# A decoder step on one Trainium2 core: the conditioning products in four column strips, their weight slots spread over the stream

## The chip, the cores and the metric

The kernel runs on one core of one Trainium2 chip. The metric is the device time of one execution in microseconds. Engines are named as the profile names them: PE (TensorE matmul; PEld its weight loads), DVE (VectorE), ACT (ScalarE), POOL (GpSimd), SP (SyncE, which issues most transfers).

## What is computed

One step of a two-layer decoder over 256 prompt tokens and 8 single-token samples (T = 264 columns), model width 1024, all in fp32. Cut to what matters here:

```python
def trunk(x, c, ret_state, past, p):
    for l in range(DEPTH):                                   # DEPTH = 2
        sh1, sc1, g1, sh2, sc2, g2 = adaln(c, p['w_mod'][l], p['b_mod'][l], 6)   # silu(c) @ w + b
        if l < N_A_LAYERS:                                   # layer 0: retention
            h = modulate(rmsnorm(x, p['g_mix'][l]), sh1, sc1)
            o, s_new = retention_mixer(h, pos, s0, p['w_ret_in'][l], p['w_ret_out'][l])
        else:                                                # layer 1: attention over shared K/V
            kv_rows, shared = build_shared_kv(x, c, past, p) # its own adaln with w_kvmod: 2 parts
            h = modulate(rmsnorm(x, p['g_mix'][l]), sh1, sc1)
            o = fox_mixer(h, shared, pos, p['w_fq'][0], p['w_fo'][0])
        x = x + g1 * o
        h = modulate(rmsnorm(x, p['g_ffn'][l]), sh2, sc2)    # modulate: h * (1 + scale) + shift
        x = x + g2 * hier_moe(h, p['w_rg'][l], p['w_re'][l], p['w_e_gate'][l], p['w_e_up'][l], p['w_e_down'][l])
    return rmsnorm(x, p['g_final']), ...
```

The conditioning vectors c (one of the prompt, eight of the samples, NC = 9) go through `w_mod[0]`, `w_mod[1]` (1024 x 6144 each) and `w_kvmod` (1024 x 2048). Of each table a part is needed only where it is used: shift and scale 1 before the mixer, gate 1 at the first residual, shift and scale 2 before the experts, gate 2 behind them. The expert mixer has 32 experts, of which each token takes two.

## The kernel before

**Weights.** All large weights lie in one stream of 296 slots (`wstream`), a slot being 128 rows of 2048 numbers, 1 MB, or 256 output columns of a 1024-row matrix. SP loads slot n into place n mod 6 of `ring` as soon as PE has begun the slot that follows slot n - 6 (`slot_used`, raised by the first matmul of each slot). PE takes the slots strictly in the order of the stream: 24 of `mod0`, then 24 of the retention projection alternating with 24 of `mod1`, then 8 of the retention output alternating with 8 of `kvmod`, 96 of the first expert block, 8 of K/V, 4 of Q, 4 of the attention output, 96 of the second expert block.

**A conditioning slot** (`mod_rows`): silu of c, feature-major in `cs` (9 columns for each of 8 row blocks), is the stationary operand, the slot's 256 columns move: eight matmuls accumulate in rows 0 to 8 of one bank. ACT copies the 9 x 256 result into one of two rows of `mrow`; `mod_turn` has PE turn it into two tiles of 128 x 9, one slot later, into bank M; `add_bias` on DVE adds the bias when all slots of a table are turned (of `mod0`, six by six). In the trace a matmul in fp32 is two records.

**Order on PE.** First stage: 24 slots of `mod0`, then the sum of squares of x (`rms`), Square on ACT before it, root on ACT and normalise and modulate on DVE behind it. Retention: Q and K (8 slots, `columns`), V (8 slots, `values`), each followed by a slot of `mod1`; sums over the past pages' forget values (DVE, `past_ready`); four heads; then 32 state steps, four in each lap of a loop over the gate projection's 8 slots. In a step PE broadcasts a value row (`value_rows`), ACT scales a state tile, DVE adds the product to it, and PE reads the state with the query (`read_state`); the third and the fourth step of a lap have one half of a `mod1` slot each between broadcast and read. The output projection (`rout`) alternates with `kvmod`.

**Routing** (`moe`): sum of squares, DVE normalise and modulate (`h_ready`), logits, transposes, DVE picks two experts (`chosen_ready`), counts and places, DVE builds the picking matrix (`pick_ready`), then 48 matmuls sort the tokens by expert into `x_sorted` (the sorting block), ACT copying each of 16 results. DVE reads the first windows' starts and copies the windows; experts are run in pairs, each expert's 64 rows in one half of the array's columns (`into_experts`, strips of 64). Layer 1's K/V/Q stage (`fk`, `fv`, `fq`) has no conditioning work; the attention over the samples' pages, bound by DVE, follows it.

**Banks.** `plan_turns` gives each product one of eight banks, in the order of the program: L[0] to L[3], X0 to X2 and M.

Of the kernel before, what the change touches and what calls it, by code (L numbers as in the profile page):

```python
# [28 lines left out]
ALU = mybir.AluOpType  # L29
# [32 lines left out]
S_MOD0, S_RET, S_RO, S_MOE0 = 0, 24, 72, 88  # L62
S_KV = S_MOE0 + 3 * NE
S_FQ = S_KV + 8
S_FO = S_FQ + 4
S_MOE1 = S_FO + 4
SLOTS = S_MOE1 + 3 * NE
# [5 lines left out]
for _name, _n in (("ident", P), ("ones", P), ("half0", P), ("half1", P), ("cosq", T), ("sinq", T),  # L73
                  ("cosk", T), ("sink", T), ("decay", RH * TP), ("kdec", 2 * RH), ("upto", TP),
                  ("causal", 3 * P), ("negeye", FH), ("eps", 1), ("first4", NG), ("first8", EG),
                  ("place", PICKS), ("before", 2 * NE), ("back", 2 * NE), ("rank", 1)):
    CONST[_name] = (_at, _n)
    _at += _n
# [41 lines left out]
def plan_turns():  # L120
    t = Turns()
    t.loop(24 // R, [(("row0", r), (X1, X2)[r % 2]) for r in range(R)] + [("mod0", M)])
    t.add(("rms", 0), X0)
    t.add("mod1", M)
# [10 lines left out]
    for i in range(16):  # L135
        t.add(("row1", i), X2)
# [7 lines left out]
    for i in range(8):  # L144
# [4 lines left out]
        t.add(("row1", 16 + i), X2)  # L149
# [5 lines left out]
    t.add("kvmod", M)  # L155
    for i in range(8):
        t.add(("row2", i), X2)
# [4 lines left out]
    def moe(l):  # L162
        t.add(("rms", 1 + 2 * l), X0)
        t.add(("logits", l), X1)
        t.add(("logitsT", l), X1)
        t.add(("count", l), X2)
        for c in range(3):
            for i in range(2):
                t.add(("ht", l, c, i), L[(2 * c + i) % 4])
        t.add(("place", l), X0)  # L170
        for k in range(KT):
            for i in range(2):
                t.add(("sorted", l, k, i), (2 * k + i) % 8)
# [17 lines left out]
    t.add("flogit", X1)  # L191
    t.add("logfT", X2)
    t.add("F", X0)
# [63 lines left out]
def build(nc, consts, x_in, c_in, vecs, wsmall, wstream, kcache, vcache, lfcache, ptable, state,  # L257
# [3 lines left out]
    with ctx:  # L261
# [21 lines left out]
        cs = sb("cs", [P, KT, NC])  # L283
# [4 lines left out]
        coef2 = sb("coef2", [P, KT, NC])  # L288
        root = sb("root", [P, T])
        rstd = sb("rstd", [P, T])  # L290
# [4 lines left out]
        arena_cols = 26600  # L295
# [22 lines left out]
        mrow = ret.take(2, 256)  # L318
# [31 lines left out]
        lgT = me.take(T, rows=36)  # L350
# [109 lines left out]
        cond_ready = sem("cond_ready")  # L460
        squared = sem("squared")
# [79 lines left out]
        def _(sp):  # L541

            sp.dma_start(cs[:], c_in).then_inc(cond_in, 16)
# [28 lines left out]
            stream(R, S_MOE0 + 3 * NE)  # L572
# [8 lines left out]
            stream(S_KV, S_MOE1 + 1)  # L581
# [5 lines left out]
            stream(S_MOE1 + 1, SLOTS)  # L587
# [118 lines left out]
        def _(pe):  # L706
# [39 lines left out]
            def rms(r):  # L746
                ps, full = begin(("rms", r))
                pe.wait_ge(squared, r + 1)
# [30 lines left out]
            def mod0_lap(it):  # L779
                for r in range(R):  # L780
                    pe.wait_ge(slot_in[r], it * 16 + 16)
                    first_of_slot[0] = not (isinstance(it, int) and r == 0)
                    mod_rows(("row0", r), r, it)
                    if r == 0 and isinstance(it, int):
                        pe.wait_ge(consts_in, 48)
                    if r == 0:
                        ps, full = begin("mod0", it)
                    else:
                        mod_turn(("row0", r - 1), (r - 1) % 2, ps, 2 * (r - 1), None, it)
                mod_turn(("row0", R - 1), (R - 1) % 2, ps, 2 * (R - 1), full, it)  # L790

            mod0_lap(0)
            with pe.Fori(1, 24 // R) as it:
                mod0_lap(it)
# [4 lines left out]
            mod1_ps, mod1_full = begin("mod1")  # L799

            def mod1_slot(i):

                take_slot(S_RET + 2 * i + 1)
                mod_rows(("row1", i), S_RET + 2 * i + 1)
                if i:
                    mod1_turn(i - 1)

            def mod1_turn(i):
                mod_turn(("row1", i), i % 2, mod1_ps, 2 * i, mod1_full if i == 23 else None)
# [14 lines left out]
            for i in range(8):  # L824
                take_slot(S_RET + 2 * i)
                for m in range(2):
                    columns(("qk", i, m), S_RET + 2 * i, m, h)
                mod1_slot(i)
            for i in range(8):
                take_slot(S_RET + 2 * (8 + i))  # L830
                values("v", "vs", S_RET + 2 * (8 + i), h, i)
                mod1_slot(8 + i)
# [86 lines left out]
            for i in range(8):  # L919
                n = S_RET + 2 * (16 + i)  # L920
# [10 lines left out]
                take_slot(n + 1)  # L931
                mod_rows(("row1", 16 + i), n + 1, None, range(0, 4))
# [1199 lines left out]
```

## Time and profile before

| | us |
|---|---|
| median of 3 runs | 1825.7 |
| lowest, highest | 1814.26, 1830.74 |
| the profiled execution | 1820.2 |
| its span in the trace | 1818.6 |

| engine | busy us | share of the span |
|---|---|---|
| PE | 1520.1 | 84% |
| PEld | 782.4 | 43% |
| DVE | 470.7 | 26% |
| ACT | 248.2 | 14% |
| POOL | 145.4 | 8% |

The share of PE is a mean over stages in which PE sets the pace and others in which transfers (the experts) or DVE (the attention) do. The mean granted TensorE clock is 0.914 of full speed. What a change is worth has to be read from the stage in which it lies.

### The profile page before, as it was taken

The numbers are of one execution on the slowest core, as the hardware profiler recorded it, in microseconds if no ns is written. First come the engines' busy times: TensorE is split into PE (matmuls) and PEld (weight loads), VectorE is DVE, ScalarE is ACT, GpSimd is POOL, SyncE is SP. The second block draws the span as 40 slices with busy tenths as digits, with TensorE's granted clock in tenths as the row PEclk, the third lists the DMA queues.
The fourth block names the chain that finished last, engine by engine and source line by source line (L and its number), as shares of the span: only waits on it lengthen the run. The fifth ranks groups of instructions, "written<-read, shape, count | busy, mean of one in ns | idle before, by whom it ended". The sixth has DMA issues, their size and how long they took to land. (4 is left out here: it accounts for less than half of the span.)

```text
span 1818.6 us, 18157 instructions
## 1 busy us (share of the span) xinstructions
PE 1520.1 (84%) x6076; PEld 782.4 (43%) x6076; DVE 470.7 (26%) x1040; ACT 248.2 (14%) x533; POOL 145.4 (8%) x242
## 2 busy tenths in 40 slices
PE   7979999999996996877775799689888968777774
PEld 3446666544444664322222577222232445222223
DVE  0021100212224015111110300876777142111102
ACT  0010000132222001100000100221221011000010
POOL 3310000011110000000001000011011000000001
PEclk9989999999998997999998899677777989999996
DMA  9755444168772550799999133466666313999982
GB/s 386 276 190 187 168 155 146 62 218 278 269 268 78 185 208 1 301 424 426 420 401 388 46 140 139 152 230 251 209 242 220 130 44 122 423 410 425 416 353 72
DMA packets 80080, 430.08 MB, mean 236 GB/s; under 512 B 12984, under 2 KB 14152, under 8 KB 41488
## 3 DMA queue, kind: packets, MB, share of 16 engines
q1 hardware_dynamic: 52560, 347.53, 49.2%
q0 software_dynamic: 26400, 76.31, 11.7%
q10 hardware_dynamic: 1056, 5.36, 0.7%
q8 instruction: 44, 0.72, 0.2%
q14 instruction: 20, 0.16, 0.0%
HBM read 402.69 MB, written 38.91 MB: 243 GB/s over the span
## 5 line engine op out<-in xcount | busy, mean ns | idle before, releaser
L710 PE MATMUL bank<-ring,arena 128*64 128x512 f32 (+2 forms) x1728 | 401.3, 585 | 117.1 <-issue 60.3
L710 PE MATMUL bank<-arena 128*16 128x512 f32 (+10 forms) x1024 | 350.8, 492 | 48.0 <-DMA arena<-y_rows,pick_ids 30.0
L710 PEld LDWEIGHTS bank<-ring,arena 128*64 128x64 f32 (+2 forms) x1728 | 153.6, 141 | 342.9 <-issue 332.6
L1276 ACT ACTIVATE arena<-bank 128x256 f32<-128x256 f32 (+8 forms) x260 | 111.3, 433 | 1008.0 <-PE bank L710 766.0
L710 PEld LDWEIGHTS bank<-arena 128*128 128x128 f32 (+4 forms) x1024 | 140.1, 167 | 217.4 <-issue 178.9
L710 PE MATMUL bank<-ring,cs 128*9 128x256 f32 x896 | 205.6, 382 | 9.8 <-DMA ring<-wstream 9.5
L710 PE MATMUL bank<-h,ring 128*128 128x264 f32 x640 | 151.5, 395 | 8.0 <-DVE h L1520 8.0
L710 PEld LDWEIGHTS bank<-h,ring 128*128 128x128 f32 x640 | 121.2, 192 | 41.5 <-issue 13.0
L710 PEld LDWEIGHTS bank<-ring,cs 128*9 128x9 f32 x896 | 77.7, 91 | 128.6 <-issue 30.8
L710 PE MATMUL bank<-arena,ring 128*128 128x264 f32 x512 | 119.4, 395 | 13.9 <-DVE arena L1606 13.0
L710 PEld LDWEIGHTS bank<-arena,ring 128*128 128x128 f32 x512 | 98.4, 194 | 32.2 <-DVE arena L1606 13.5
L710 PE MATMUL bank<-arena,cst 16*128 16x128 f32 (+9 forms) x204 | 75.0, 483 | 29.7 <-DVE arena L1963 19.8
L1784 DVE TENSOR_TENSOR arena<-bank,arena 128x256 f32<-128x256 f32 x32 | 13.6, 424 | 290.4 <-ACT arena L1386 290.4
L710 PE MATMUL bank<-ring,h 128*128 128x256 f32 (+1 forms) x384 | 85.8, 381 | 0.0
L1592 DVE SCALAR_TENSOR_TENSOR arena<-bank,arena 128x512 f32<-128x512 f32 x64 | 45.1, 746 | 144.9 <-PE bank L710 115.8
L641 POOL DMA_INDIRECT y_rows<-arena,dest_ids x32 | 31.0, 969 | 619.7 <-DVE arena L1771 536.6
L1898 DVE TENSOR_TENSOR h<-arena,xn 128x1024 f32<-128x1024 f32 x64 | 77.3, 1217 | 0.6
L1902 DVE TENSOR_REDUCE arena<-h 128x16 f32<-128x1024 f32 x64 | 76.8, 1211 | 0.0
L624 POOL DMA_DIRECT2D arena<-vcache x64 | 34.1, 533 | 519.6 <-PE bank L710 392.2
L710 PE MATMUL bank<-xn,cst 128*128 128x264 f32 (+1 forms) x144 | 63.3, 571 | 11.9 <-ACT xn L1297 11.9
L710 PEld LDWEIGHTS bank<-ring,h 128*128 128x128 f32 (+1 forms) x384 | 58.8, 156 | 23.1 <-issue 2.7
L710 PEld LDWEIGHTS bank<-arena,cst 16*128 16x128 f32 (+4 forms) x204 | 40.7, 237 | 60.5 <-issue 46.5
(209 smaller groups left out, 722.2 us busy)
## 6 DMA issues: line engine op xcount, KB each, us to landing
ring<-wstream SPq DMA_DIRECT2D x296, 1024.0 KB, 8.7
arena<-vcache POOLq DMA_DIRECT2D x64, 512.0 KB, 4.9
arena<-kcache SPq DMA_DIRECT2D x64, 512.0 KB, 4.6
arena<-state POOLq DMA_DIRECT2D x32, 512.0 KB, 6.6
ss_out<-arena POOLq DMA_DIRECT2D x32, 512.0 KB, 5.5
sp_out<-arena ACTq DMA_DIRECT2D x4, 512.0 KB, 2.8
cst<-consts SPq DMA_DIRECT2D x1, 1963.0 KB, 9.0
x<-x_in SPq DMA_DIRECT2D x1, 1056.0 KB, 21.5
```

What stands on the lines that cost most here:

```text
L624: pool.dma_start(ring_[:, r, :], cache[ds(page, 1)].rearrange("a p n -> p (a n)")).then_inc(sems[r], 16)
L641: nc.gpsimd.indirect_dma_start(y_rows[0:PICKS], bass.IndirectOffsetOnAxis(dest_ids[:, p:p + 1], 0), y_sb[:, p % 2, :], None, bounds_check= ...
L710: ins = nc.tensor.matmul(out, w, rhs, start=start, stop=stop, skip_group_check=True)
L1276: return nc.scalar.activation(out, in_, ACT.Copy)
L1592: ins = stt(st[:, u % 4, s, :], ps[:], qk[:, 8 + 2 * hd + s, TP + b:TP + b + 1], st[:, u % 4, s, :], ALU.mult, ALU.add)
L1784: tt(aff[:, p % 2, :], ps[:, FF:2 * FF], act_g[:, p % 2, :], ALU.mult).then_inc(free(("GU", l, p)), 1)
L1898: tt(prod[:, j % 2, :], kpg[:, j % 4, :], qb, ALU.mult).then_inc(k_used, 1)
L1902: step(nc.vector.tensor_reduce(sc[:, j * FH:(j + 1) * FH], prod[:, j % 2, :].rearrange("p (h d) -> p h d", h=FH), AX, ALU.add))
```

## The change

The conditioning product of a slot is laid out in four strips of 32 output rows: row block k accumulates in rows 32 (k mod 4) to 32 (k mod 4) + 31 of the bank, so that each strip holds the sum of two blocks, and `cs` is padded with zeros to 32 columns. ACT copies all 128 rows. The turn multiplies the copied rows with a constant matrix (`strips`, ones where row mod 32 is the column), which adds the four strips and turns them in one matmul for each tile of 128 columns.

The order of the stream is new. Eight slots of `mod0` (shift and scale 1) lead. Twelve (gate 1, shift and scale 2) follow one after every second slot of the retention projection. The remaining four of `mod0`, all eight of `kvmod` and the first eight of `mod1` stand between the output projection and the first expert block; `WAITS` sets them in the routing's waits: two behind the projection, five before the logits, two before the counts, three before the sorting, eight in the sorting block. Twelve of `mod1` alternate with the K, V and Q slots, four stand in the second routing (one and three). `add_bias` works once for each such part. `mrow` moves out of the arena, the raw c shares `coef2`, `rstd` shares `root`, `lgT` lies in `x_sorted`; the sorted results use seven banks, since M collects the turns; `rms` waits for Square before it takes its bank.

```diff
+def stream_order():
+    order = [("mod0", i) for i in range(8)]
+    for i in range(24):
+        order.append(("ret", i))
+        if i % 2:
+            order.append(("mod0", 8 + i // 2))
+    order += [("ro", i) for i in range(8)]
+    order += [("mod0", 20 + i) for i in range(4)] + [("kvmod", i) for i in range(8)] + [("mod1", i) for i in range(8)]
+    order += [("moe0", i) for i in range(3 * NE)]
+    for i in range(12):
+        order += [("kv", i) if i < 8 else ("fq", i - 8), ("mod1", 8 + i)]
+    order += [("fo", i) for i in range(4)] + [("mod1", 20 + i) for i in range(4)]
+    return order + [("moe1", i) for i in range(3 * NE)]
...
+WAITS = ((2, 5, 2, 3, 8), (1, 3, 0, 0, 0))
+STRIP = 32
...
-        cs = sb("cs", [P, KT, NC])
+        cs = sb("cs", [P, KT, STRIP])
...
-            def mod_rows(key, n, it=None, blocks=range(KT)):
-
+            def fill_rows(part, i, blocks=range(KT)):
+
+                n = SLOT[PARTS[part][i]]
+                if blocks[0] == 0:
+                    take_slot(n)
+                key = ("row", part, i)
                 w = slot(n)
-                b, _ = turn(key, it)
-                ps, full = begin(key, it) if blocks[0] == 0 else (bank[b], filled[b])
+                b, _ = turn(key)
+                ps, full = begin(key) if blocks[0] == 0 else (bank[b], filled[b])
                 for k in blocks:
-                    mm(ps[0:NC, 0:256], cs[:, k, :], w[:, k, :], k == 0, k == KT - 1,
+                    strip = slice(STRIP * (k % 4), STRIP * (k % 4) + STRIP)
+                    mm(ps[strip, 0:256], cs[:, k, :], w[:, k, :], k < 4, k >= 4,
                        full if k == KT - 1 else None)
 
-            def mod_turn(key, buf, ps, tile, done=None, it=None):
-
-                moved(pe, key, it)
+            def fill_turn(part, i):
+
+                if i < 0:
+                    return
+                if i == 0:
+                    begin(part)
+                moved(pe, ("row", part, i))
                 for m in range(2):
-                    turned(ps[:, (tile + m) * NC:(tile + m + 1) * NC], mrow[0:NC, buf, m * P:(m + 1) * P], NC,
-                           m == 0, done if m else None)
+                    tile = 2 * i + m
+                    ins = nc.tensor.matmul(bank[M][:, tile * NC:(tile + 1) * NC], mrow[:, i % 2, m * P:(m + 1) * P],
+                                           c_("strips"), start=True, stop=True, skip_group_check=True)
...
+            def fill(part, i):
+
+                fill_rows(part, i)
+                fill_turn(part, i - 1)
...
             def moe(l, base):
...
+                fill_wait(0)
                 rms(1 + 2 * l)
+                fill_wait(1)
                 pe.wait_ge(h_ready, 2 + 3 * l)
...
+                fill_wait(2)
                 pe.wait_ge(chosen_ready, l + 1)
...
+                fill_wait(3)
                 pe.wait_ge(pick_ready, l + 1)
...
+                    if k < WAITS[l][4]:
+                        fill(part, next(fills))
+                    if k == max(WAITS[l][4] - 1, 0):
+                        fill_turn(part, len(PARTS[part]) - 1)
...
                 ins.then_inc(gates_ready, 1)
+                add_bias(f"route{l}")
```

PE in the Q and K stage, the first two slots before. `ring,cs` is the product of a conditioning slot, `h,ring` the projection, the rows of L725 and L727 are a turn:

```order
L710 MATMUL bank0<-h,ring 128x264 x8
L710 MATMUL bank1<-h,ring 128x264 x8
L710 MATMUL bank6<-ring,cs 9x256 x8
L710 MATMUL bank2<-h,ring 128x264 x8
L710 MATMUL bank3<-h,ring 128x264 x8
L710 MATMUL bank6<-ring,cs 9x256 x8
L725 MATMUL bank7<-cst,arena 128x9
L727 MATMUL bank7<-cst,arena 128x9
```

The same place now, the third and fourth slot (L833 is the new turn):

```order
L760 MATMUL bank0<-h,ring 128x264 x8
L760 MATMUL bank1<-h,ring 128x264 x8
L760 MATMUL bank2<-h,ring 128x264 x8
L760 MATMUL bank3<-h,ring 128x264 x8
L760 MATMUL bank6<-ring,cs 32x256 x8
L833 MATMUL bank7<-cst,mrow 128x9 x2
```

A conditioning product stands behind every second projection slot instead of every one, with 32 rows for 9.

PE from the end of the output projection (`arena,ring`) to the logits (`h,wsm`) before; `xn,cst` is the sum of squares:

```order
L710 MATMUL bank2<-arena,ring 128x264 x8
L710 MATMUL bank3<-arena,ring 128x264 x8
L710 MATMUL bank6<-ring,cs 9x256 x8
L725 MATMUL bank7<-cst,arena 128x9
L727 MATMUL bank7<-cst,arena 128x9
L725 MATMUL bank7<-cst,arena 128x9
L727 MATMUL bank7<-cst,arena 128x9
L710 MATMUL bank4<-xn,cst 128x264 x8
L710 MATMUL bank5<-h,wsm 36x264 x8
```

And now, up to the first of the five fills ahead of the logits:

```order
L760 MATMUL bank2<-arena,ring 128x264 x8
L760 MATMUL bank3<-arena,ring 128x264 x8
L760 MATMUL bank0<-ring,cs 32x256 x8
L760 MATMUL bank1<-ring,cs 32x256 x8
L833 MATMUL bank7<-cst,mrow 128x9 x2
L760 MATMUL bank4<-xn,cst 128x264 x8
L760 MATMUL bank2<-ring,cs 32x256 x8
L833 MATMUL bank7<-cst,mrow 128x9 x2
```

The conditioning slots between the parts of the output projection are gone, and seven others stand before and behind the sum of squares.

PE at the end of the first sorting block (`arena` alone) and the start of the experts (`ring,arena`) before:

```order
L710 MATMUL bank4<-arena 128x264 x3
L710 MATMUL bank5<-arena 128x264 x3
L710 MATMUL bank6<-arena 128x264 x3
L710 MATMUL bank7<-arena 128x264 x3
L710 MATMUL bank0<-ring,arena 64x512 x16
```

And now:

```order
L760 MATMUL bank5<-arena 128x264 x3
L760 MATMUL bank6<-arena 128x264 x3
L760 MATMUL bank2<-ring,cs 32x256 x8
L833 MATMUL bank7<-cst,mrow 128x9 x2
L760 MATMUL bank0<-arena 128x264 x3
L760 MATMUL bank1<-arena 128x264 x3
L760 MATMUL bank3<-ring,cs 32x256 x8
L833 MATMUL bank7<-cst,mrow 128x9 x4
L760 MATMUL bank0<-ring,arena 64x512 x16
```

A fill stands behind every two sorted results, and the last turn stands right before the experts.

## Rows read from the trace of the kernel before

**Rows 1.** Busy us by stage: PE, PEld, DVE, ACT, POOL; granted clock, DMA share, GB/s.

```profile
15.00:35.00 20.00, 19.81 (x96) 8.77 (x97) 0.00 (x0) 1.86 (x5) 7.09 (x14) 1.00 1.02 414
...
371.50:557.60 186.10, 184.91 (x616) 80.60 (x615) 45.67 (x67) 44.36 (x62) 31.92 (x60) 1.00 0.76 262
...
581.50:676.00 94.50, 92.92 (x408) 63.77 (x408) 5.89 (x19) 4.83 (x9) 1.59 (x4) 0.97 0.50 182
...
676.00:737.70 61.70, 42.69 (x183) 32.62 (x183) 26.15 (x101) 13.05 (x29) 0.53 (x1) 0.81 0.08 28
...
737.70:996.40 258.70, 184.85 (x800) 64.82 (x800) 27.85 (x62) 21.98 (x49) 20.21 (x21) 0.95 0.99 412
...
1032.35:1134.20 101.85, 101.48 (x457) 78.69 (x456) 3.85 (x10) 11.44 (x27) 0.00 (x0) 1.00 0.40 145
```

**Rows 2.** The page, parts 5 and 6: conditioning matmuls; the load of x.

```profile
L710 PE MATMUL bank<-ring,cs 128*9 128x256 f32 x896 | 205.6, 382 | 9.8 <-DMA ring<-wstream 9.5
...
x<-x_in SPq DMA_DIRECT2D x1, 1056.0 KB, 21.5
```

**Rows 3.** Timeline of PE, first stage: start, us, instruction, records.

```profile
15.10 3.61 PE L710 MATMUL bank<-ring,cs 128*9 128x256 f32 x16 [3.12 <-DMA ring<-wstream]
...
18.64 0.39 PE L725 MATMUL bank<-cst,arena 9*128 9x9 f32 x2
...
19.02 3.62 PE L710 MATMUL bank<-ring,cs 128*9 128x256 f32 x16
```

**Rows 4.** Timeline of PE: a full-width block; a block of experts.

```profile
369.62 1.98 PE L710 MATMUL bank<-arena 128*128 128x512 f32 x4 [1.79 <-ACT arena L1276]
...
805.26 3.65 PE L710 MATMUL bank<-ring,arena 128*64 128x512 f32 x16 [1.25 <-DMA ring<-wstream]
...
808.85 0.44 PE L1029 MATMUL bank<-cst,arena 128*128 128x128 f32 x2
```

**Rows 5.** Timeline of SP, start: the issue of x.

```profile
6.23 0.44 SPq L550 DMA_DIRECT2D x<-x_in  x1
```

**Rows 6.** Timeline of PE: from the sum of squares to the first projection.

```profile
108.01 5.51 PE L710 MATMUL bank<-xn,cst 128*128 128x264 f32 x16 [1.41 <-ACT xn L1297]
...
121.52 9.82 PE L710 MATMUL bank<-h,ring 128*128 128x264 f32 x32 [8.00 <-DVE h L1520]
```

**Rows 7.** Timeline, end of the value projections: PE, and the past sums on DVE.

```profile
325.51 3.62 PE L710 MATMUL bank<-ring,cs 128*9 128x256 f32 x16
...
328.65 0.29 DVE L1553 TENSOR_TENSOR arena<-arena 128x128 f32<-128x128 f32 x1
```

**Rows 8.** Timeline, one state step of four: DVE's update, PE's read behind it.

```profile
385.94 1.41 DVE L1592 SCALAR_TENSOR_TENSOR arena<-bank,arena 128x512 f32<-128x512 f32 x2 [5.21 <-PE bank L710]
...
387.56 1.88 PE L710 MATMUL bank<-arena 128*8 128x512 f32 x4
...
390.53 1.41 DVE L1592 SCALAR_TENSOR_TENSOR arena<-bank,arena 128x512 f32<-128x512 f32 x2 [3.18 <-PE bank L710]
...
392.62 1.88 PE L710 MATMUL bank<-arena 128*8 128x512 f32 x4
```

**Rows 9.** Timeline, end of the output projection: last conditioning slot, Square, sum of squares.

```profile
670.03 3.62 PE L710 MATMUL bank<-ring,cs 128*9 128x256 f32 x16
...
673.97 1.95 ACT L1297 ACTIVATE xn<-x 128x2112 f32<-128x2112 f32 x1
...
676.06 5.47 PE L710 MATMUL bank<-xn,cst 128*128 128x264 f32 x16 [1.50 <-ACT xn L1297]
```

**Rows 10.** Timeline of PE, first routing: what follows each wait (in brackets).

```profile
690.16 5.18 PE L710 MATMUL bank<-h,wsm 128*36 128x264 f32 x16 [8.63 <-DVE h L1520]
...
701.96 0.95 PE L710 MATMUL bank<-cst,arena 128*32 128x128 f32 x6 [2.97 <-DVE arena L1679]
...
712.12 24.02 PE L710 MATMUL bank<-arena 128*128 128x264 f32 x96 [4.88 <-DVE arena L1694]
...
737.68 10.52 PE L710 MATMUL bank<-ring,arena 128*64 128x512 f32 x48 [1.54 <-issue]
```

More of the change, by code:

```diff
@@ L75 @@
                   ("causal", 3 * P), ("negeye", FH), ("eps", 1), ("first4", NG), ("first8", EG),
-                  ("place", PICKS), ("before", 2 * NE), ("back", 2 * NE), ("rank", 1)):
+                  ("place", PICKS), ("before", 2 * NE), ("back", 2 * NE), ("rank", 1), ("strips", NC)):
     CONST[_name] = (_at, _n)
@@ L121, in plan_turns @@
     t = Turns()
-    t.loop(24 // R, [(("row0", r), (X1, X2)[r % 2]) for r in range(R)] + [("mod0", M)])
+    t.add("first", M)
+    t.add("ret", M)
+    for i in range(8):
+        t.add(("row", "first", i), (X1, X2)[i % 2])
     t.add(("rms", 0), X0)
-    t.add("mod1", M)
     for i in range(8):
@@ L134, in plan_turns @@
     t.add("past_total", X0)
-    for i in range(16):
-        t.add(("row1", i), X2)
+    for i in range(8):
+        t.add(("row", "ret", i), X2)
     for h in range(RH):
@@ L162, in moe, with rows @@
     def moe(l):
+        fills = iter(range(len(PARTS[f"route{l}"])))
+        def rows(at_wait):
+            for _ in range(WAITS[l][at_wait]):
+                i = next(fills)
+                t.add(("row", f"route{l}", i), L[i % 4])
+        t.add(f"route{l}", M)
+        rows(0)
         t.add(("rms", 1 + 2 * l), X0)
+        rows(1)
         t.add(("logits", l), X1)
@@ L169, in moe @@
                 t.add(("ht", l, c, i), L[(2 * c + i) % 4])
+        rows(2)
         t.add(("place", l), X0)
+        rows(3)
+        extra = WAITS[l][4]
         for k in range(KT):
             for i in range(2):
-                t.add(("sorted", l, k, i), (2 * k + i) % 8)
+                t.add(("sorted", l, k, i), (2 * k + i) % 7)
+            if k < extra:
+                i = next(fills)
+                t.add(("row", f"route{l}", i), L[i % 4])
         def out(p):
@@ L191, in plan_turns @@
     t.add("flogit", X1)
+    t.add("attend", M)
+    for i in range(4):
+        t.add(("row", "attend", i), X2)
     t.add("logfT", X2)
+    for i in range(4, 12):
+        t.add(("row", "attend", i), X2)
     t.add("F", X0)
@@ L1279, in _, with fill, rms @@
             act.wait_ge(cond_in, 16)
[L1280 removed]
+            nc.scalar.activation(cs[:, :, 0:NC], c_raw[:], ACT.Silu).then_inc(cond_ready, 1)
             act.wait_ge(consts_in, 48)
             eps = c_("eps")
[L1284 to L1292 removed]
+            def fill(part, i):
+                key = ("row", part, i)
+                ps = result(act, key)
+                copy(mrow[:, i % 2, :], ps[:, 0:256]).then_inc(free(key), 1)
+            for i in range(8):
+                fill("first", i)
+            def rms(r, meanwhile=None):
                 if r == 0:
@@ L1302, in _ @@
             rms(0)
-            for i in range(8):
-                mod_rows(("row1", i), i % 2)
+            for i in range(4):
+                fill("ret", i)
             for i in range(8):
@@ L1347, in _, with fill_wait @@
                     .then_inc(free(("gn", hd)), 1)
-            for i in range(8):
-                mod_rows(("row2", i), i % 2)
             def moe(l):
-                rms(1 + 2 * l)
+                part = f"route{l}"
+                fills = iter(range(len(PARTS[part])))
+                def fill_wait(at_wait):
+                    for _ in range(WAITS[l][at_wait]):
+                        fill(part, next(fills))
+                rms(1 + 2 * l, fill_wait)
+                fill_wait(1)
                 ps = result(act, ("logits", l))
@@ L1368, in moe @@
                         copy(x_sorted[:, k, i * T:(i + 1) * T], ps[:, 0:T]).then_inc(free(("sorted", l, k, i)), 1)
+                    if k < WAITS[l][4]:
+                        fill(part, next(fills))
                 def half_out(p):
```

204 lines of the change are left out of this document (105 added, 99 removed).

## The prediction

> **What bounds the kernel now.** I read the table by stages first, then the timeline of PE in the stages that the change touches, then what DVE and ACT do where PE waits. The table [rows 1] shows three kinds of stage. PE is all but full in the conditioning, retention, output-projection and K/V/Q stages (184.91 of 186.10 us in the state stage, 92.92 of 94.50 in the output projection, 101.48 of 101.85 in K/V/Q), while DMA is half idle there. The expert stage is the reverse: DMA share 0.99 at 412 GB/s, PE 184.85 of 258.70. The first routing is neither: DMA share 0.08, PE 42.69 of 61.70, with PE waiting for short chains on ACT and DVE. So what is removed from PE in the first kind counts in full, unless another engine is waited for in its shade; what is added to PE in a routing wait is free up to the length of the wait; and bytes moved out of one stage into another cost nothing as long as the expert stage is not made to wait for them.
>
> The conditioning product is 896 records of 205.6 us [rows 2], that is 56 slots of 16 records. One slot takes 3.62 us, and from one slot's start to the next 3.92 us [rows 3]: 16 records at 0.216 us make 3.46, and 0.46 is left for the three records that turn the previous slot's rows.
>
> **The price of a slot in four strips (a fill).** The trace has no block in four strips, but it has one in two. A full-width block pays 1.98 us for four records of 512 columns, about 0.43 each and a tail [rows 4]; 16 of them in a row would take 7.1. The expert block has 16 records of 512 columns in two strips of 64 rows and takes 3.65 us [rows 4], which is 8 x 0.43 and a tail: two strips run side by side. If four do so too, 16 records of 256 columns are four rounds of 0.216, 0.86 us. The turn now has four records instead of three: 4 x 0.15 = 0.61. **A fill costs 1.5 us.** Two abreast would be 8 x 0.216 + 0.61 = 2.3, none abreast 3.46 + 0.61 = 4.1; these are the ends. I take 1.5, because the nearest row, the expert block, reaches the whole factor that its strips allow.
>
> After the expert block the next full-width matmul starts at 808.85, while the block's own row ends at 808.91 [rows 4]: no pause is seen between strips and full width. The Trainium skill, TensorEngine Tiling (Array Packing), section Tiling Modes (Key Properties), says that a change of tiling mode drains TensorE, and each fill here makes two such changes. By that rule, with an estimated 0.2 us for each drain, the 28 fills that lie on the path would cost 11 us more; the row speaks against it, and the sum leaves it out.
>
> **The change, stage by stage.** *First stage.* 24 slots become 8. With 1.5 us a fill PE now waits for DMA: x is issued at 6.23 [rows 5] behind six slots and lands 21.5 us later [rows 2], at 27.7; the two remaining slots follow at 1.05 MB / 414 GB/s [rows 1] = 2.53 us each, so the eighth is there at 32.8. Its fill ends at 33.8, ACT's copy at 34.3, Square (1.95 us [rows 9]) at 36.3. From the sum of squares to the first projection it is 121.52 - 108.01 = 13.5 us as before [rows 6], so that starts at 49.8 instead of 121.52. Should PE run at the lower level up to there, 2.5 us are lost; I take **-71**.
>
> *Q/K and values.* 16 slots go (16 x 3.92 = 62.7), 8 fills come (12.0). At the end the last slot covered DVE's sums over the past pages: they end at 328.94, 3.4 us after the slot's start [rows 7]; a fill covers 1.5 of it, so 1.9 come back. **-48.8.**
>
> *State steps.* Eight slots were cut in two halves, each set between a value broadcast and the read that waits for DVE. The first read starts at 387.56, and DVE's update ended at 387.35 [rows 8]: the half was hidden, nothing is won. The second starts at 392.62, DVE's update ended at 391.94: 0.6 us are won, eight times 4.8 at most; nothing at least, if the state's loads are late next. The four fills that stay hide in the same place. **-4**, from 0 to -5.
>
> *Output projection.* Eight slots leave. Seven count 3.92. The last one held ACT's queue: Square started only at 673.97, behind that slot's copy, though the projection's last matmul was done at 670.03, and the sum of squares came at 676.06 [rows 9]. Now it is the residual's 0.9 us on DVE and Square's 1.95 after the projection, at 673.1: 2.9 more. **-30.**
>
> *First routing.* Twenty fills come here, 20 MB of weights into a stage that has DMA share 0.08 [rows 1]. Twelve of them stand in waits: two behind the projection (3.0 us until Square is done), five before the logits (8.63 us), two before the counts (2.97) and three before the sorting (4.88) [rows 10]; 3.0, 7.5, 3.0 and 4.5 us of fills just fit. Eight stand in the sorting block, which has no wait: +12. Behind it DVE now adds the biases of three tables and only then reads the starts of the first windows, which used to happen under the sorting: the last row's copy 0.4, its turn 0.6, and the adds and reads on DVE, together between 1.5 and 4 us, 2.5 taken. Against that, three blocks ran partly at the lower clock level after their waits (the granted clock of the stage is 0.81 [rows 1]): 5.47 and 5.18 us for 16 records and 24.02 for 96 [rows 9, 10], where 0.223 us a record (0.216 x 264/256) gives 3.6, 3.6 and 21.4, 6 us in all. Fills keep PE at work before them; I take half, 3 us, with 0 and 6 as ends. **+11.5.**
>
> *Experts.* Before and after, the ring holds five expert slots when the block starts, for the sixth waits for the first one's use. No change.
>
> *K/V/Q.* Twelve fills come into a stage in which PE is full [rows 1]: 12 x 1.5, and 0.4 for one add on DVE. **+18.4**, 28.5 with two abreast. *Second routing:* four fills, one and three, in waits of the same lengths: nothing.
>
> **Sum:** -71 - 48.8 - 4 - 30 + 11.5 + 18.4 = -123.9 us, against the profiled execution's 1820.2: 1696. The three runs' median, 1825.7, lies 5.5 above that execution, in the middle of a spread of 16; I put a third of it on top: **1698 us**.
>
> **The rivals.** (1) *Only two strips run abreast*, a fill is 2.3. The 28 fills on the path (8, 8 and 12) cost 0.84 more each, 23.5; the routing's waits overflow by 1.7, 3.1, 1.7 and 2.1; together +32: 1730. For it: no block in four strips is in the trace, and each matmul here is a pair of records. Against it: had the pairs gone strictly one behind the other, the expert block would have shown a ninth round, 4.1 us; it shows 3.65 [rows 4]. The Trainium skill, TensorE: Matmul & The Clock Gate, Part 3 (The mechanism), has matmuls start and end strictly in the program's order, which with two records on the same strip next to each other gives this rival; on the two strips the row does not bear it out.
>
> (2) *Strips run one after another*, a fill is 4.1, more than a nine-row slot. 28 x 2.57 = 72 on the path, 29 beyond the first routing's waits, 5 beyond the second's, 10 in the first stage, less 2: +114, 1812, no change that a measurement shows. The expert block speaks against it.
>
> (3) *Slower than before: each record of a fill waits for the one before it to leave the array*, strip by strip. A record alone lasts 382 ns [rows 2], so a fill is 16 x 0.382 + 0.61 = 6.7. Between 2.3 and 4.1 each microsecond of a fill costs 47 in all; past 4.4 us a fill the change loses, and at 6.7 it stands at 1937. Nothing in the trace shows 32-row strips alternating at such a price, but nothing shows the opposite either.
>
> (4) *The expert weights come late.* If the twenty slots push the five leading expert slots behind the start of that stage, it starts 5 x 2.53 = 12.7 us late: 1711. The fills of the sorting block come 4.2 us apart and a slot needs 2.53, which speaks against it.
>
> **How the numbers follow.** Forecast 0.68 (its own ends 1682 and 1714: state 0 to -5, routing 6 to 17, clock in the first stage, and some 8 us between runs), two abreast 0.16, late weights 0.06, strips one after another 0.05, slower 0.03, something else 0.02. The range 1676 to 1736 takes in the forecast, the late weights and the greater part of the second case, and leaves out the rest, about 0.2. A measurement here cannot tell 1% from nothing. Faster by over 1%: 0.93; within: 0.04; slower: 0.03.
>
> **What would show it.** In the profile after: fills of about 1.0 us with rows of 128x256 in 32 rows, and turns near 0.6; the first projection near 50 us; the value stage at 10.6 us a slot with every second one 1.5 longer; state steps as long as before within 1 us per four; waits of 0.5 us or less before logits, counts and sorting; the experts at 258 us. A fill of 2 us or above, a routing that grew by more than 17 us, or an expert stage longer than 260 us would make it wrong.

## The result, and the profile after

| us | before | after |
|---|---|---|
| median of 4 runs | 1826.7 | 1740.74 |
| lowest, highest | 1814.26, 1830.74 | 1725.33, 1744.4 |
| the profiled execution | 1820.2 | 1739.59 |
| its span | 1818.6 | 1738.1 |
| mean granted clock of TensorE | 0.914 | 0.887 |

The ratio of the times is 0.9533, with a 95% interval of 0.9498 to 0.9567: faster by 4.7%. The prediction was 1698, in a range of 1676 to 1736; the median lies 4.7 us above that range.

The table by stages of the kernel after, with the columns of [rows 1], in order: first stage; Q/K, values and heads; state steps; output projection; first routing; experts; K/V/Q.

```profile
0.00:52.45 52.45, 28.33 (x176) 16.52 (x176) 7.79 (x16) 8.23 (x13) 16.62 (x35) 0.97 0.83 333
52.45:252.30 199.85, 193.79 (x951) 139.88 (x951) 31.96 (x93) 19.35 (x47) 20.80 (x39) 0.98 0.40 147
252.30:467.65 215.35, 196.17 (x549) 81.65 (x548) 46.16 (x69) 45.12 (x60) 31.93 (x60) 0.82 0.60 207
...
489.78:552.41 62.63, 61.16 (x292) 51.07 (x293) 6.99 (x19) 2.51 (x3) 0.74 (x2) 0.97 0.41 144
552.41:629.32 76.91, 70.84 (x547) 47.76 (x547) 25.38 (x104) 20.11 (x47) 1.38 (x3) 0.89 0.77 294
629.32:891.29 261.97, 187.12 (x800) 66.10 (x801) 27.87 (x62) 21.82 (x48) 20.77 (x22) 0.95 0.98 407
...
927.82:1046.20 118.38, 118.00 (x687) 87.98 (x686) 3.97 (x11) 15.65 (x38) 0.00 (x0) 1.00 0.62 223
```

The state steps of the kernel before, in the same view and cut by the same rule (first broadcast to first sum of the group norm):

```profile
371.54:559.43 187.89, 185.26 (x621) 80.92 (x620) 46.38 (x69) 45.50 (x64) 31.92 (x60) 1.00 0.75 260
```

Against the kernel before, cut at the same instructions, the first stage went from 121.52 to 52.45 us, the Q/K, value and head stage from 250.0 to 199.85, the output projection from 94.5 to 62.63, the first routing from 61.6 to 76.91, the experts from 258.8 to 261.97, K/V/Q with the attention behind it from 405.7 to 426.55. Each of these is within 4 us of its term. The state steps are not: they lost PE work and went **from 187.89 to 215.35**. Their PE busy time rose too, from 185.26 to 196.17, though the trace has 72 records fewer, and the granted clock fell from 1.00 to 0.82. Instructions that take longer each are the mark to look for.

The price of a fill. The page after has all 896 records in 73.6 us instead of 205.6 [rows 2]:

```profile
L760 PE MATMUL bank<-ring,cs 128*32 128x256 f32 x896 | 73.6, 436 | 15.7 <-DMA ring<-wstream 15.6
```

The timeline of PE after, two fills of the first routing, then the last fill of the first stage, the sum of squares and the first projection:

```profile
556.15 1.07 PE L760 MATMUL bank<-ring,cs 128*32 128x256 f32 x16
...
557.69 1.07 PE L760 MATMUL bank<-ring,cs 128*32 128x256 f32 x16
...
34.51 1.94 PE L760 MATMUL bank<-ring,cs 128*32 128x256 f32 x16
...
38.80 5.67 PE L760 MATMUL bank<-xn,cst 128*128 128x264 f32 x16 [0.55 <-ACT xn L1364]
...
52.45 2.13 PE L760 MATMUL bank<-h,ring 128*128 128x264 f32 x4 [7.99 <-DVE h L1609]
```

A fill and a turn take 1.54 us from start to start (556.15 to 557.69) where it was 3.92 [rows 3]: four strips abreast, as priced. At the lower level its rows take 1.94. All eight fills of the first stage have that length (the view's granted clock reads 1.00 from 15 to 39 us all the same, so only the length of the rows shows it); the sum of squares came at 38.80, and the first projection 13.65 us behind it, as before [rows 6].

A lap of state steps after: the third and fourth step of the first lap (no fill), then the second lap (fill halves in its third and fourth step). In brackets, the wait and what ended it:

```profile
266.70 1.41 DVE L1681 SCALAR_TENSOR_TENSOR arena<-bank,arena 128x512 f32<-128x512 f32 x2 [5.21 <-PE bank L760]
...
268.16 3.40 PE L760 MATMUL bank<-arena 128*8 128x512 f32 x4 [1.50 <-DVE arena L1681]
...
274.12 3.08 PE L760 MATMUL bank<-arena 128*8 128x512 f32 x4 [1.50 <-DVE arena L1681]
...
279.12 6.67 PE L760 MATMUL bank<-h,ring 128*128 128x264 f32 x16
285.72 1.88 PE L760 MATMUL bank<-arena 128*8 128x512 f32 x4
...
296.78 1.88 PE L760 MATMUL bank<-arena 128*8 128x512 f32 x4 [0.93 <-DVE arena L1681]
...
301.22 2.87 PE L760 MATMUL bank<-arena 128*8 128x512 f32 x4 [0.39 <-DVE arena L1681]
```

The broadcast is done, DVE's update takes 1.41 us, and PE waits 1.50 for it where the half of a nine-row slot used to stand [rows 8]; the next step the same; in the second lap the waits are 0.93 and 0.39. The steps' waits are those that the prediction read. But from the first wait on instructions appear at the lower level: the read of four records takes 3.40 and 3.08 instead of 1.88, sixteen projection records 6.67 instead of 3.83.

The first routing after (start of each block behind a wait, fills ahead of the sorting, the last turns, the first expert), beside [rows 10]:

```profile
551.97 0.58 PE L833 MATMUL bank<-cst,mrow 128*128 128x9 f32 x4 [1.47 <-ACT mrow L1343]
552.41 3.81 PE L760 MATMUL bank<-xn,cst 128*128 128x264 f32 x16
...
564.86 3.75 PE L760 MATMUL bank<-h,wsm 128*36 128x264 f32 x16 [0.92 <-DVE h L1609]
...
579.42 1.93 PE L760 MATMUL bank<-ring,cs 128*32 128x256 f32 x16
...
587.80 5.04 PE L760 MATMUL bank<-arena 128*128 128x264 f32 x12
...
623.97 1.19 PE L833 MATMUL bank<-cst,mrow 128*128 128x9 f32 x8
629.32 12.36 PE L760 MATMUL bank<-ring,arena 128*64 128x512 f32 x48 [4.16 <-issue]
```

Sum of squares and logits take 3.81 and 3.75 us instead of 5.47 and 5.18. The fills alone do not decide that: in e2_split, e4_tail and e6_both (below), which have the same fills there, the logits took 5.44, and in b1_thin and b2_bare (below), which have none, the sum of squares took 3.80. Three things cost PE time. It waits 1.47 for ACT's copy ahead of the last turn behind the projection (in the row of the output projection). The three fills ahead of the sorting run at the lower level (1.93 us for the rows of the first), 579.42 to 587.80, 8.4 us in a wait of 4.88 [rows 10]. And behind the last turn PE stands still for 4.16 until the first window is there, where it was 1.54 [rows 10]; the first 48 records of the experts behind it take 12.36 us instead of 10.52.

### The profile page after: what moved, and what is told of

The parts are those of the page before. It is cut to its first block and busy times, and to the rows that moved or that the text cites. A ratio compares the mean times of both kernels' runs of the same rounds, so it can differ in the third digit from the quotient of the medians.

```text
span 1738.1 us, 18249 instructions
## 1 busy us (share of the span) xinstructions
PE 1436.0 (83%) x6132; PEld 754.2 (43%) x6132; DVE 470.8 (27%) x1042; ACT 249.6 (14%) x533; POOL 145.6 (8%) x242
## 5 line engine op out<-in xcount | busy, mean ns | idle before, releaser
L760 PE MATMUL bank<-arena 128*16 128x512 f32 (+10 forms) x1024 | 368.9, 510 | 59.3 <-DMA arena<-y_rows,pick_ids 30.4
L1343 ACT ACTIVATE arena<-bank 128x256 f32<-128x256 f32 (+5 forms) x204 | 90.4, 450 | 600.0 <-PE bank L760 371.0
L760 PE MATMUL bank<-h,ring 128*128 128x264 f32 x640 | 161.1, 413 | 8.0 <-DVE h L1609 8.0
L760 PEld LDWEIGHTS bank<-h,ring 128*128 128x128 f32 x640 | 128.3, 204 | 47.2 <-issue 15.8
L760 PEld LDWEIGHTS bank<-arena,ring 128*128 128x128 f32 x512 | 97.9, 192 | 31.2 <-DVE arena L1695 12.7
L760 PE MATMUL bank<-arena,cst 16*128 16x128 f32 (+9 forms) x204 | 77.7, 497 | 31.5 <-DVE arena L2053 19.9
L760 PE MATMUL bank<-ring,cs 128*32 128x256 f32 x896 | 73.6, 436 | 15.7 <-DMA ring<-wstream 15.6
L760 PE MATMUL bank<-xn,cst 128*128 128x264 f32 (+1 forms) x144 | 71.1, 628 | 8.3 <-ACT xn L1364 8.3
L1860 DVE COPY arena<-bank 128x512 f32<-128x512 f32 x32 | 22.1, 691 | 142.0 <-PE bank L760 142.0
## 6 DMA issues: line engine op xcount, KB each, us to landing
x<-x_in SPq DMA_DIRECT2D x1, 1056.0 KB, 22.9
```

The costliest lines, as they stand in the source:

```text
L760: ins = nc.tensor.matmul(out, w, rhs, start=start, stop=stop, skip_group_check=True)
L1343: return nc.scalar.activation(out, in_, ACT.Copy)
L1860: nc.vector.tensor_copy(y_sb[:, p % 2, 512:D], ps[:]).then_inc(free(("Y", l, p, 1)), 1)
```

## The experiments

**Theory:** the state steps are longer because PE's waits for DVE, which the nine-row halves had covered, let the clock fall to 1.2 GHz; data come no later than before. **Rival:** something is late (state loads, ACT's scaling, DVE), or the strips themselves do it, and the clock is a by-product.

**1. Useless work in the waits** (e1_warm), and half of it (e7_half, with `range(2)`).

```diff
+            def warm(row):
...
+                for k in range(4):
+                    nc.tensor.matmul(bank[X2][0:STRIP, 0:256], cs[:, k, :], h[:, k, 0:256], ...)
...
                 if i % 2:
                     fill_rows("ret", 8 + i // 2, range(0, 4))
+                else:
+                    warm(8 + i // 2 - 1)
```

> The changed kernel with one addition: in the even laps of the state steps, where PE waits for DVE twice, four matmuls on constants into an unused bank take the place of the wait (rows of 256 columns in one strip, about 1.9 us, as long as the half slots of the kernel before; their result is read by nobody). Theory (clock): the state stage is longer because PE's waits let its clock fall to the lower level. Then the useless work makes the kernel faster: granted clock of the stage 0.95 or more, reads of four records back at 1.88 and projections at 3.83 us, the stage 185 to 192 us instead of 215.35, the whole about 1712. Rival (data): the steps wait for state loads or for DVE; then the stage stays at 215 or grows by the added work, the whole 1740 or more.

> The changed kernel with half of the useless work of the first run: two matmuls instead of four in each of the two waits of the even laps, so that about 0.6 us of each wait of 1.5 is left. If a wait of this length is short enough for the clock, the stage has 184 to 187 us and a granted clock of 0.97 or more; if only a closed wait helps, 195 to 210 us.

Measured: e1_warm 1709.37 us (1706.49 to 1712.4), ratio to before 0.938, interval 0.9343 to 0.9417; e7_half 1712.0 in one run. The state stage of e1_warm, and the third step of its first lap:

```profile
252.69:439.05 186.36, 178.59 (x613) 77.83 (x612) 46.16 (x69) 44.71 (x60) 31.91 (x60) 0.98 0.68 240
...
266.99 1.91 PE L974 MATMUL bank<-h,cs 128*32 128x256 f32 x8
268.74 1.88 PE L760 MATMUL bank<-arena 128*8 128x512 f32 x4
```

The same of e7_half:

```profile
253.58:438.50 184.92, 172.97 (x581) 73.97 (x580) 46.16 (x69) 44.50 (x60) 31.93 (x60) 0.98 0.71 241
...
269.44 1.88 PE L760 MATMUL bank<-arena 128*8 128x512 f32 x4 [0.52 <-DVE arena L1693]
```

With matmuls that compute nothing the kernel is some 30 us faster than the changed kernel (0.938 of the kernel before, against 0.9533). The stage is back at 186.36 us with a clock of 0.98; half the useless work, with 0.52 of each wait left, does as well in its one run. Nothing of the data's way was touched, so data are not what is late: that part of the rival falls. All of the 29 us between 215.35 and 186.36 is the clock, since a step with a wait of 1.50 at the full clock is no longer than one with the useless work in its place: 4.44 us in b2_bare below (from the broadcast at 385.88 to the next at 390.32), 4.61 here (265.94 to 270.55), against 5.95 in the changed kernel (265.54 to 271.49).

**2. The kernel before with its cover thinned** (b1_thin) **and taken out** (b2_bare).

```diff
b1_thin
-                mod_rows(("row1", 16 + i), n + 1, None, range(0, 4))
+                mod_rows(("row1", 16 + i), n + 1, None, range(0, 4) if i % 2 else range(0, 1))
...
-                mod_rows(("row1", 16 + i), n + 1, None, range(4, 8))
+                mod_rows(("row1", 16 + i), n + 1, None, range(4, 8) if i % 2 else range(7, 8))
...
b2_bare: both halves only if i % 2; in even laps, behind the last read,
...
+                    for done in (None, full):
+                        mm(ps[0:NC, 0:NC], cs[:, 0, :], cs[:, 0, :], True, True, done)
```

> The kernel before with work taken away: in the even laps of the state steps each half of the nine-row slot has one product of four (four slots lose six of their eight products, so four slots of the second conditioning table are wrong). Some 12 us of PE work go. Theory (clock): the waits that this opens twice in every second lap let the clock fall; the state stage gets longer than its 187.89 us, 200 to 215, and the kernel as a whole slower by 10 to 27. Rival (data): the stage stays at 188 or falls by up to 3, since those halves only hid the wait for DVE.

> The kernel before with the nine-row slots of the even laps of the state steps taken out (two tiny products of nine columns behind the lap's last read stand for each; four slots of the second conditioning table are wrong), so that PE waits twice, some 1.5 us each, in every second lap, as in the changed kernel, while the odd laps keep their half slots. Theory (clock): though about 14 us of PE work are gone, the stage grows from 187.89 us to between 200 and 215, with a granted clock of 0.82 to 0.92, and the whole by 12 to 27 us. Rival (the fall of the clock in the changed kernel comes from the strips or from something else in it): the stage stays at 185 to 188 us at clock 1.00, the whole 0 to 3 us faster.

Measured: b1_thin 1830.93 us (1821.37 to 1838.5), ratio 1.0044, interval 1.0018 to 1.007; b2_bare 1837.06 (1834.22 to 1839.37), ratio 1.0072, interval 1.005 to 1.0095. The stage of b1_thin, the seventh of its eight laps, in which the clock fell most (0.93 in the third, 1.00 in the others), and the waits of its first lap:

```profile
370.73:561.29 190.56, 182.25 (x572) 77.31 (x571) 46.36 (x69) 45.74 (x64) 31.98 (x60) 0.96 0.74 256
...
514.00:538.00 24.00, 22.75 (x53) 7.64 (x53) 5.48 (x9) 4.76 (x7) 3.20 (x6) 0.79 0.70 248
...
386.59 1.88 PE L710 MATMUL bank<-arena 128*8 128x512 f32 x4 [0.97 <-DVE arena L1592]
...
391.03 1.88 PE L710 MATMUL bank<-arena 128*8 128x512 f32 x4 [0.60 <-DVE arena L1592]
```

The stage of b2_bare, and the two reads behind a wait in its first lap:

```profile
372.64:571.94 199.30, 184.63 (x572) 81.70 (x571) 46.38 (x69) 45.14 (x64) 31.93 (x60) 0.93 0.71 245
...
388.50 1.88 PE L710 MATMUL bank<-arena 128*8 128x512 f32 x4 [1.50 <-DVE arena L1600]
...
392.94 3.31 PE L710 MATMUL bank<-arena 128*8 128x512 f32 x4 [1.50 <-DVE arena L1600]
```

Both lost PE work and became slower, by 0.4% and 0.7%, with no 32-row strip in the program: so it does not take the strips. b2_bare's stage grew by 11.4 us, from 187.89 to 199.30, and the whole by 11.8. (Behind this stage the second layer of both works with a table that is partly wrong, so the stage is the measure more than the whole.) b1_thin, with waits of 0.97 and 0.60, missed what was expected of its stage: 190.56 in the profiled execution, not 200 to 215 (its median rose by more, 8.5 us, and the profiled execution is one of its shorter ones; where the rest lies is not shown).

The seven kernels side by side, each from its window of the stage and the waits in brackets in its first two laps:

| kernel | waits of PE for DVE's state updates, us | clock | stage, us |
|---|---|---|---|
| e2_split (below) | none (0.76 once, in the first step) | 1.00 | 166.61 |
| before | none | 1.00 | 187.89 |
| e1_warm | 0.93, 0.39 | 0.98 | 186.36 |
| e7_half | 0.52, 0.52, 0.93, 0.39 | 0.98 | 184.92 |
| b1_thin | 0.97, 0.60 | 0.96 | 190.56 |
| b2_bare | 1.50, 1.50 | 0.93 | 199.30 |
| after | 1.50, 1.50, 0.93, 0.39 | 0.82 | 215.35 |

The changed kernel is b2_bare with waits in the odd laps as well. Either set alone costs less: the waits of the even laps 11.4 us (b2_bare), and with those of the odd laps alone the clock keeps 0.98 (e1_warm). That both together make up the whole 27.5 us is read from this table; no run puts the odd laps' waits into the kernel before.

**3. Real work in the waits** (e2_split): the gate projection of a lap, two blocks of 3.83 us, becomes four of half the length, one for each step.

```diff
-                value_rows(4 * i) ... columns(("g", i, 0), n, 0, h) ... read_state(4 * i)
-                value_rows(4 * i + 1) ... columns(("g", i, 1), n, 1, h) ... read_state(4 * i + 1)
...
+                for u in range(4):
+                    value_rows(4 * i + u)
+                    if u == 0:
+                        take_slot(n)
+                    columns(("g", i, u // 2), n, u // 2, h, blocks=range(4 * (u % 2), 4 * (u % 2) + 4))
...
+                    if u == 3 and i % 2:
+                        fill("ret", 8 + i // 2)
+                    read_state(4 * i + u)
```

> The changed kernel with the gate projections cut in halves: each of the four state steps of a lap gets half a projection (1.9 us) between the value broadcast and the read, instead of two steps with a whole one and two with little; fills stand in the last step of odd laps. Theory (clock and cover): no wait of PE for DVE is left, the clock stays at the upper level, a step is 1.12 + 1.92 + 1.88 = 4.92 us, 32 of them 157, with fills and turns of outputs 165 us instead of 215.35, the whole about 1690. If the clock alone came back and the waits stayed: 185. Rival (data): at under 5.5 us a step the state loads or ACT's scaling come late, the stage stays above 185 us with waits for them before DVE's updates.

Measured: 1688.64 us (1687.78 to 1689.55), ratio 0.9273, interval 0.9237 to 0.9309. Its state stage, and one step (half a projection, then the read, without a bracket):

```profile
251.75:418.36 166.61, 163.38 (x550) 69.75 (x549) 46.16 (x69) 44.27 (x60) 31.94 (x60) 1.00 0.77 268
...
263.31 2.05 PE L760 MATMUL bank<-h,ring 128*128 128x264 f32 x8
265.28 1.88 PE L760 MATMUL bank<-arena 128*8 128x512 f32 x4
...
263.41 1.41 DVE L1674 SCALAR_TENSOR_TENSOR arena<-bank,arena 128x512 f32<-128x512 f32 x2 [3.43 <-PE bank L760]
```

A step is 4.84 us (from one projection's start, 263.31, to the next at 268.15), the stage 166.61, 165 expected. Its 550 records keep PE busy for 163.38 us; the 549 of the changed kernel, the same work, kept it busy for 196.17. The update on DVE ends at 264.82, the read starts at 265.28 when the projection is through. The rival's late loads don't appear at this pace either.

**4. The gap ahead of the experts** (e4_tail), and both edits in one kernel (e6_both).

```diff
                 ins.then_inc(gates_ready, 1)
-                add_bias(f"route{l}")
...
                 for p in range(2):
                     take_windows(p, first_two[p])
+                add_bias(f"route{l}")
```

> The changed kernel with one order on DVE turned round, in both routings: the first four windows are read and copied first, the biases of the conditioning tables are added after them. Theory: in the first routing the adds, the last turn and the four register reads (629.32 less 624.1, about 5 us) stand between the last sorting copy and the first expert; with the other order the reads go under the last fill and the expert block starts 3 to 4.5 us sooner after the last sorting matmul. The whole 1736 to 1740 if the expert stage starts sooner and ends sooner; no change of the whole if the weights' transfers alone set the end of that stage (its length then grows by as much as its start came forward).

> The split gate projections and the turned order on DVE (windows first, biases after) in one kernel. If both gains are where the single runs showed them, they add: 1688.6 less 4 to 5 us of the gap ahead of the experts, about 1684. If the expert stage's end is set by its transfers alone, the start that comes 4 us sooner is given back inside the stage and the whole stays at 1688.

Measured: e4_tail 1733.51 in one run, which alone tells nothing beside the changed kernel's 1725 to 1744. Its rows do: the first routing, the experts, and the end of the sorting block:

```profile
553.47:626.35 72.88, 70.98 (x547) 47.57 (x547) 25.22 (x102) 19.41 (x47) 1.38 (x3) 0.91 0.76 296
626.35:886.07 259.72, 182.33 (x801) 64.07 (x801) 28.02 (x64) 22.52 (x49) 20.93 (x22) 0.97 1.00 415
...
625.23 1.19 PE L833 MATMUL bank<-cst,mrow 128*128 128x9 f32 x8
626.35 10.52 PE L760 MATMUL bank<-ring,arena 128*64 128x512 f32 x48
```

The gap of 4.16 us is gone: the first expert starts as the last turn ends. The routing is 72.88 instead of 76.91, and the expert stage is not longer for it but 2.25 shorter. Its first 48 records take 10.52 us again, 1.84 less than behind the wait of 4.16. The expert stage takes 261.1 to 262.0 us in the four kernels that have this wait (the changed one, e1_warm, e2_split, e7_half), 259.7 and 259.9 in the two that lost it (e4_tail, e6_both). e6_both: 1681.71 us (1679.07 to 1687.84), ratio 0.9225, interval 0.9182 to 0.9268; its stages of the first routing, the experts and the sum behind them (the first two cut 0.1 to 0.2 us ahead of their first matmuls):

```profile
504.63:577.55 72.92, 71.02 (x548) 47.66 (x547) 25.27 (x102) 19.33 (x47) 1.54 (x3) 0.91 0.79 298
577.55:837.58 260.03, 183.91 (x803) 64.51 (x802) 28.16 (x64) 22.67 (x49) 20.76 (x22) 0.96 1.00 413
837.58:873.60 36.02, 25.20 (x128) 19.50 (x128) 14.27 (x41) 5.01 (x4) 0.39 (x1) 0.71 0.06 20
```

In the rows the two gains stand side by side: 72.92 us for the routing, without the gap, in the kernel with the split projections. By the time it is 7 us faster than e2_split, as expected, but the intervals of the two overlap.

**5. Eight fills from a full stage into a wait** (e8_late): the eight slots of the second table leave the sorting block.

```diff
-    order += [("moe0", i) for i in range(3 * NE)]
+    order += [("moe0", i) for i in range(3 * NE)] + [("mod1", i) for i in range(8)]
...
-WAITS = ((2, 5, 2, 3, 8), (1, 3, 0, 0, 0))
+WAITS = ((2, 5, 2, 3, 0), (1, 3, 0, 0, 0))
...
                 out_of_experts(PAIRS - 1)
+                if l == 0:
+                    for i in range(8):
+                        fill("late", i)
+                    fill_turn("late", 7)
```

> The kernel before this one in the list with one more move: the eight slots of the second conditioning table leave the sorting block of the first routing and go behind the last expert, where PE waits 17.9 us for the gathered expert rows. Theory (a fill costs 1.5 us on a full PE and nothing in a wait that is long enough): the first routing loses 12 us, the wait takes eight fills (12.3 us), the whole is 1672. Rival (bytes): their 8.4 MB come at 2.53 us a slot behind the last expert weights, some 20 us, and share the DMA engines with the gather; then the sum of the experts starts up to 8 us later and the whole is 1676 to 1684.

Measured: 1675.96 us (1671.61 to 1679.32), ratio 0.918, interval 0.9139 to 0.922, which overlaps that of e6_both. By stages, cut as those of e6_both, and PE at the start of the sum:

```profile
505.41:566.64 61.23, 57.79 (x387) 41.36 (x387) 24.72 (x101) 16.86 (x39) 1.38 (x3) 0.89 0.58 231
566.64:831.35 264.71, 201.50 (x960) 75.52 (x961) 28.54 (x65) 25.06 (x57) 21.07 (x22) 0.96 1.00 415
831.35:868.23 36.88, 24.63 (x129) 19.21 (x129) 14.27 (x41) 5.01 (x4) 0.00 (x0) 0.75 0.39 155
...
812.47 1.07 PE L765 MATMUL bank<-ring,cs 128*32 128x256 f32 x16 [1.39 <-DMA ring<-wstream]
...
826.42 1.94 PE L765 MATMUL bank<-ring,cs 128*32 128x256 f32 x16
831.35 5.95 PE L765 MATMUL bank<-arena 128*128 128x128 f32 x32 [1.19 <-DMA arena<-y_rows,pick_ids]
838.73 7.31 PE L765 MATMUL bank<-arena 128*128 128x128 f32 x64 [1.43 <-DMA arena<-y_rows,pick_ids]
```

The first routing lost 11.7 us (72.92 to 61.23), 1.46 for each fill as a net figure: without the fills the wait of 1.54 ahead of the first expert is back, and some blocks ran at another level (the logits 3.75 instead of 5.44). The expert stage, with the wait behind it, became 4.7 longer and the sum 0.9. The first fills wait for their slots (1.39 us at 812.47), the later ones run at the lower level, and PE is done with the last turn at 830.17. In e6_both the sum starts 259.9 us after the first expert; here that would have been 826.5. So 3.6 us of the delay are PE's own, and 1.19 more it waits for the gathered rows.

The theory of a free wait is wrong. The bytes have a part in it and the clock another; they were not taken apart. The median lies at the lower edge of what the bytes' account expected. It is the fastest kernel of the study by its median, 65 us under the changed one; the two profiled executions, of e6_both and of this kernel, are only 2.6 us apart, since the stages behind the sum took 2.8 longer in this one, which the edit does not explain.

## Why the prediction was wrong

The sum was 1696 for an execution that took 1739.6. Of the 43.6 us between them 31.5 are one term; the other 12 are spread over the stages below. None of the four rivals had this case; it fell under "something else", 0.02.

**The step that failed: state steps, -4, from 0 to -5; measured +27.5.** "The half was hidden, nothing is won" was read rightly from [rows 8] as far as DVE goes: the waits came out as these rows say. But the step put the price of the opened waits at nothing, and that was not so. Work that nobody waits for kept PE busy, and the kernel before has a clock of 1.00 there. Take it out and PE waits 1.50 us twice in every second lap (0.93 and 0.39 in the others), the clock falls to 0.82, and everything in the stage that PE does, which is nearly all, takes longer. Experiment 1 shows it from the changed kernel; experiment 2 shows it from the kernel before, with 11.4 of the 27.5 us. With the clock kept, the term would have come out: the 184.92 of e7_half is 3.0 under the kernel before. The prediction asked what would cover the work that it added; it did not ask what the removed work had itself been the cover of. The Trainium skill, TensorE: Matmul & The Clock Gate, Part 1 (A second HAM failure mode: psum-queue depth-cycling), reports of another kernel, in bf16, that short idle times of PE between groups of matmuls made its clock swing between the two levels; the rows of this stage agree (clock 0.82, records of one kind at both lengths).

**The price of a fill, 1.5: right.** 1.54 from start to start where PE was at the upper level, and 1.47 between two results of the sorting block (592.77 to 594.24). So rivals 1 to 3 are out: two abreast would have been 2.3.
**First stage, -71; measured -69.1.** The fills were as long as at the lower level there, x landed after 22.9 us instead of 21.5, and the first projection came at 52.45 instead of 49.8.

**Q/K and values, -48.8; measured -50.2** (with the heads). **Output projection, -30; measured -31.9.** Right.

**First routing, +11.5; measured +15.3,** inside the ends of 6 to 17 (7.5 to 16 by its own terms). Mis-sized were above all the three fills ahead of the sorting, taken as fitting, which ran over by 3.5 us at the lower level. The tail behind the sorting came to 3.2 (a turn of 0.6, and a wait of 4.16 for one of 1.54) where 2.5 was taken. Sum of squares and logits gained 3.1 through the clock where 3 was taken; by the other runs above that was partly luck.

**Experts, 0; measured +3.2.** Late weights, rival 4 with 12.7 us, did not happen. 1.84 us stand in its first 48 records, which run partly at the lower level behind the wait of 4.16; 2.25 went with that wait in e4_tail. How the start of a stage bound by transfers reaches its end is not shown.

**K/V/Q, +18.4; measured +18.4** from its first projection to the attention's first product (101.33 to 119.75 us; the row of the table ends inside the last fill), and 2.4 more in the attention behind it. There the first matmuls run at the lower level after the change; this was not tested by itself. **Second routing, 0; measured +3.1** (59.77 to 62.84), not tested either.

## What to carry to other kernels

As this case shows, work in the shade of another engine is free to remove only if PE has something else to do there: read the granted clock of the stage before, and ask which waits the removal opens and how often they come back. A stage in which PE waits a little in every step is better served by cutting the work that is there anyway into pieces of the length of the wait (49 us here, against 29 for useless work) than by moving work out. And work that is moved into a wait is free only if its bytes arrive in time and PE is at the upper clock there: eight fills that cost 11.7 us in a full stage still cost 5.5 in a wait of 17.8.

## What the runs showed of the hardware

Four strips of 32 rows run abreast although each fp32 matmul is two records: 16 records of 256 columns take 1.07 us, against 3.62 in one strip [rows 3], and no pause is seen between strips and full width.

Taking PE work out of a stage lengthened it: an estimated 14 us less work in b2_bare (eight halves of 1.9, less four stand-ins of 0.3), 11.4 us more time. Putting useless work in shortened it by 29. The clock of the changed kernel's stage fell to 0.82 though PE was busy for 196.17 of 215.35 us; the kernel with the same two waits in every second lap and none in the others kept 0.93.
